# A two-block transformer kernel on one core: no masked quarter in the window attention, projections placed inside other waits, and 24 instead of 20 up projections ahead of the one-hot rounds

## The chip, the cores and the metric

One core of a Trainium2 chip runs the whole program in one launch. The metric is the time of the device from start to end of that launch, in microseconds (us), as the median of several runs. The engines are TensorE (PE, with its weight loads as PEld), VectorE (DVE), ScalarE (ACT), GpSimd (POOL) and SyncE (SP), which here only issues transfers.

## The reference, cut to what matters

All tensors are float32, 256 tokens, width 1024. Two blocks follow each other.

```
first block:  h = x + gmlp(rms_norm(x))                 # u, v, g: 3 x 2048 columns; v mixed over time; 2048 -> 1024
              k, v = split(rms_norm(h) @ w_kv + b_kv)    # 2 key/value heads of 64, k with rotary
              q, g = split(rms_norm(h) @ w_in)           # 16 query heads of 64
              scores: 128-token chunks, keys of the own and the previous chunk,
                      key valid if 0 <= q - k < 128;  m = max(scores, sink)
              p = exp(s - m) / (sum + exp(sink - m));  h += (p @ v * silu(g)) @ w_out
              h = rms_norm(h, final)
second block: h1 = rmsnorm(h) * (1 + sc1) + sh1          # sc, sh, g from silu(c) @ ada_w + ada_b
              q, k, v = h1 @ w_in; 16 heads of window and dilated attention with a bias table
              h += g1 * (rmsnorm(o) @ w_out)
              peer(h2): q = h2 @ wq, two 128-key scores per head, top 16 x 16 -> top 16 of 8 heads
                        a = h2 . u[id],  w = gate * gelu(a),  y = sum of w * v[id] over 16384 experts
              out = rmsnorm(h + g2 * y)
```

## The kernel before, in words

Activations are kept with features on the partitions and the 256 tokens in the free dimension. All weights come in one stream of 128 x 1024 float32 chunks (512 KB), through a ring of four slots `raw`, `WH`, `WL`. SP loads a chunk; `hi` on ACT (L397) copies it, rounded, to WH; `lo` on DVE (L799; `pool_low` on POOL, L1539, for some) writes the rest, raw - WH, to WL. Slot c is written again once chunk c - 4 is finished. Each product is three products of halves, hi x hi, hi x lo, lo x hi. `feature_tile` (L1567) does one chunk: 8 k-slices x 3 matmuls = 24 matmuls of 256 tokens, with the weight as the stationary side. `token_tiles` (L1567 too) has the activations as the stationary side and gives tokens on the partitions. Each engine's order is written out by hand; waits are counts on semaphores (`up(c, g, per)` is such a count in a loop).

The stages in order, with their names in the code:

- `ug_step`, `aout_step`: the first mixer. `aout_step` ends with the residual x and, for each k-slice, the gained inputs X1 (for keys and values) and X2 (for queries).
- Keys and values: chunk C_KV by `feature_tile` into keys, the sum of squares by `spread` (a plain float32 product with ones), chunk C_KV + 1 by `token_tiles`, `rms` on DVE, `rope_in`/`rope_out`, `vB`.
- `swa_step(m)`, m = 0..10, one pair of heads each, skewed: PE makes the query tile (bank m % 2), `scores` of pair m - 1 (L1694), `values` of pair m - 2 (L1716), the gate tile, `rope_turn`, `turn_probs` of pair m - 1 (L1706) and `turn_out` of pair m - 2. DVE has `soft_in`: scale and mask (L995), the maximum (L1000), three operations on 4 columns (L1004, L1006, L1009). ACT has `exps` (L511) and `pt_out` (L521). Scores are 128 x 256 for each head and each half of the queries; queries of the first half have no key in the second.
- `out_steps`: w_out, 8 chunks (C_BOUT). Then `spread` of two sums of squares (POOL adds the squares, L1514), the norm on DVE, `modulated`: F = x * gain * R and X1H/X1L.
- `v2_step`: the values of the second block, 8 chunks (C_V2), as token tiles into vC. `mix_step(m)`: as `swa_step`, with keys of their own and a bias table, then C_COUT, C_WQ with the key scores and DVE's `top16`.
- `early_up` (PE), `early_step` (ACT, hi and Gelu): the first TOP = 20 up projections of the 128 columns of experts. DVE in this time makes the lists of chosen experts; ACT has one Exp for their gates (L691). `lists_ready` lets PE turn the lists (L1920).
- 32 rounds: 8 one-hot products (L1934) and one up projection each. Then EARLY = TOP + 32 down projections (`down`, L1953), then LATE = 128 - EARLY columns, each an up (L1967, L1969) and a down projection.

## Time and profile before

| what | value |
|---|---|
| median of 3 runs | 1405.53 us (1404.94 to 1407.23) |
| profiled execution, its own time | 1403.09 us |
| its span | 1401.3 us |
| PE, DVE, ACT, POOL busy | 94%, 71%, 54%, 27% |
| mean granted clock of TensorE | 0.969 of full speed |
| transfers | 249.21 MB, 177 GB/s read over the span |

Busy is the share of the span in which an engine had an instruction of the program under way. Matmuls overlap, so a mean time of one is longer than the distance from one to the next. The granted clock is 1 where TensorE ran at 2.4 GHz, 0.5 where at 1.2 GHz.

### The profile page before, as it was taken

Reading aid. Unit: us, or ns where it says so; the run is one execution under the profiler, and the core shown is the slowest. Engines: PE = TensorE matmul, PEld = TensorE weight load, DVE = VectorE, ACT = ScalarE, POOL = GpSimd, SP = SyncE. Lnnn points to the kernel's source line nnn. Section 1 sums busy time; section 2 is a strip of 40 time slices with the busy share of each in tenths; the row PEclk is TensorE's granted clock in tenths of the full one; section 3 lists DMA queues with packets and bytes.
Section 4 is the critical chain, followed back from the end, with each engine's and each line's share of the span. In section 5 each row is a group of like instructions: output and inputs, shape, how many; then the busy total and the mean of one; then the engine's idle time right before and its main releaser. Section 6 shows DMA issues by size and latency. Waiting matters only on the chain.

```text
span 1401.3 us, 26798 instructions
## 1 busy us (share of the span) xinstructions
PE 1314.0 (94%) x8582; PEld 1184.8 (85%) x8582; DVE 997.7 (71%) x1847; ACT 760.5 (54%) x1260; POOL 372.7 (27%) x252
## 2 busy tenths in 40 slices
PE   6999998997789888998999999999999999999996
PEld 6999998887689788998999967777888888888885
DVE  6799988884567686797788845555666666666666
ACT  6344453554445545545988844444555555555553
POOL 1089812112231024786777700000000000000000
PEclk9999999998899889998999999999999999999998
DMA  9877784442365533453333345555756556565561
GB/s 337 316 247 263 242 271 164 141 151 79 130 196 186 175 106 136 160 178 127 110 118 111 116 151 180 180 180 180 240 184 192 191 181 189 188 192 181 192 188 67
DMA packets 68024, 249.21 MB, mean 178 GB/s; under 512 B 7808, under 2 KB 8192, under 8 KB 67200
## 3 DMA queue, kind: packets, MB, share of 16 engines
q1 hardware_dynamic: 58896, 214.80, 46.5%
q10 hardware_dynamic: 9072, 33.69, 7.1%
q8 instruction: 33, 0.54, 0.2%
q14 instruction: 23, 0.19, 0.1%
HBM read 245.83 MB, written 2.62 MB: 177 GB/s over the span
## 4 chain that ended last, share of the span: by engine, by line
PE 81%; DVE 9%; ACT 4%; issue 3%; DMA 2%; POOL 1%; ACTq 0%; DVEq 0%; SPq 0%; POOLq 0%
PE ps L1567 30%; PE ps L1953 26%; PE ps L1967 10%; PE ps L1969 5%; PE ps L1934 4%; ACT pr L511 2%; PE ps L1706 1%; DVE small L1000 1%; DVE s L995 1%; PE ps L1842 1%; DMA ada<-adaT 1%; DVE WL L799 1%; PE ps L1716 1%; DMA raw<-stream 1%; PE ps L1694 1%
## 5 line engine op out<-in xcount | busy, mean ns | idle before, releaser
L799 DVE TENSOR_TENSOR WL<-raw,WH 128x1024 fp32r<-128x1024 f32 x326 | 412.3, 1268 | 174.7 <-ACT WH L397 171.6
L397 ACT ACTIVATE WH<-raw 128x1024 fp32r<-128x1024 f32 x394 | 414.4, 1055 | 178.1 <-PE ps L1953 85.3
L1567 PE MATMUL ps<-X,WH 128*128 128x256 f32 x1840 | 347.3, 290 | 6.1 <-DVE X2L L919 4.1
L1567 PEld LDWEIGHTS ps<-X,WH 128*128 128x128 f32 x1840 | 292.1, 196 | 7.3 <-DVE X2L L919 4.3
L1567 PE MATMUL ps<-X,WL 128*128 128x256 f32 x920 | 263.5, 286 | 0.0
L1967 PE MATMUL ps<-X,WH 128*128 128x512 f32 x608 | 216.9, 397 | 0.0
L1953 PE MATMUL ps<-WH,wvH 128*128 128x512 f32 x512 | 207.5, 405 | 2.6 <-DVE wvL L1337 2.4
L1953 PE MATMUL ps<-WH,wvL 128*128 128x512 f32 x512 | 202.5, 396 | 0.0
L1953 PE MATMUL ps<-WL,wvH 128*128 128x512 f32 x512 | 202.0, 395 | 0.0
L1539 POOL TENSOR_TENSOR WL<-raw,WH 128x1024 fp32r<-128x1024 f32 x68 | 164.0, 2413 | 82.5 <-ACT WH L397 82.5
L1567 PEld LDWEIGHTS ps<-X,WL 128*128 128x128 f32 x920 | 179.1, 195 | 0.0
L1969 PE MATMUL ps<-X,WL 128*128 128x256 f32 x608 | 170.5, 280 | 0.0
L1967 PEld LDWEIGHTS ps<-X,WH 128*128 128x128 f32 x608 | 114.2, 188 | 27.6
L1953 PEld LDWEIGHTS ps<-WH,wvH 128*128 128x128 f32 x512 | 96.9, 189 | 39.7 <-DVE wvL L1337 15.6
L1969 PEld LDWEIGHTS ps<-X,WL 128*128 128x128 f32 x608 | 114.7, 189 | 2.9
L1953 PEld LDWEIGHTS ps<-WH,wvL 128*128 128x128 f32 x512 | 96.5, 188 | 22.4
L1953 PEld LDWEIGHTS ps<-WL,wvH 128*128 128x128 f32 x512 | 96.8, 189 | 17.4
L747 ACT ACTIVATE tmp<-tmp 128x256 f32<-128x256 f32 x76 | 31.7, 418 | 107.2 <-DVE tmp L1346 107.2
L1354 DVE TENSOR_TENSOR tmp<-tmp,A 128x256 f32<-128x256 f32 x76 | 32.3, 425 | 51.9 <-ACT tmp L747 51.9
L1567 PE MATMUL ps<-WH,X 128*128 128x256 f32 (+1 forms) x352 | 64.4, 284 | 3.6 <-DVE WL L799 3.6
L1567 PE MATMUL ps<-YH,WH 128*128 128x256 f32 x224 | 64.1, 286 | 3.0 <-DVE YL L882 3.0
L807 DVE CUSTOM_DVE_ANT_0 ada<-ada,cb 128x1024 f32<-128x1024 f32 x48 | 60.7, 1265 | 6.7 <-DMA ada<-adaT 3.5
(262 smaller groups left out, 2185.6 us busy)
## 6 DMA issues: line engine op xcount, KB each, us to landing
raw<-stream SPq DMA_DIRECT2D x394, 512.0 KB, 3.4
ada<-adaT ACTq DMA_DIRECT2D x48, 512.0 KB, 4.2
bias<-att_bias ACTq DMA_DIRECT2D x9, 512.0 KB, 4.5
x<-xT SPq DMA_DIRECT2D x2, 512.0 KB, 6.7
ws<-wsT SPq DMA_DIRECT2D x1, 1024.0 KB, 11.6
lng<-rows SPq DMA_DIRECT2D x1, 1024.0 KB, 8.1
lnb<-rows SPq DMA_DIRECT2D x1, 1024.0 KB, 7.1
bsb<-rows SPq DMA_DIRECT2D x1, 1024.0 KB, 8.1
```

The costliest lines, as they stand in the source:

```text
L397: act.activation(WH[:, slot, :], raw[:, slot, :], ACT.Copy).then_inc(h_done, 1)
L511: act.activation(pr[:, k, :], s[:, k, :], ACT.Exp, bias=negm[:, k:k + 1], accum_out=small_den[:, par, k:k + 1]).then_inc(p_ready, 1)
L747: act.activation(tmp[i % 2][:, :], tmp[i % 2][:, :], ACT.Gelu).then_inc(gelu_ready, 1)
L799: dve.tensor_tensor(WL[:, slot, :], raw[:, slot, :], WH[:, slot, :].bitcast(F32), ALU.subtract).then_inc(l_done, 1)
L807: dve.tensor_tensor_reduce(ada[:, n % 2, :], ada[:, n % 2, :], cb[:, :], 1.0, 0.0, ALU.mult, ALU.add, st2).then_inc(ada_sum, 1)
L1354: dve.tensor_tensor(tmp[2 + i % 2][:, :].unsqueeze(1), tmp[i % 2][:, :].unsqueeze(1), tiles(A, EARLY + i, g, 2), ALU.mult).then_inc(w_read ...
L1539: pool.tensor_tensor(WL[:, slot, :], raw[:, slot, :], WH[:, slot, :].bitcast(F32), ALU.subtract).then_inc(l_done, 1)
L1567: mm = pe.matmul(out_ap, a(kc), b(kc), start=(first and kc == 0 and i == 0), stop=(last and kc == KC - 1 and i == 2))
L1934: mm = pe.matmul(ps[:, gate_bank(e) + half, k * P:(k + 1) * P], O1[:, n, :], (O2a, O2b[:, e % 2])[half][:, k, :], start=True, stop=True)
L1953: mm = pe.matmul(ps[:, 4 + 2 * t + h, :], a[:, j % 2, ts_], b[:, slot, hs], start=(first and i == 0), stop=(last and i == 2), skip_group_c ...
L1967: pe.matmul(ps[:, i % 2, :].rearrange("p (x t) -> p x t", x=2), wh(kc), X1[:, :, kc, :], start=(kc == 0), stop=False, skip_group_check=True)
L1969: mm = pe.matmul(ps[:, i % 2, 0:T], wl(kc), X1H[:, kc, :], start=False, stop=(kc == KC - 1), skip_group_check=True)
```

## The change

It has six parts.

1. `TOP` is 24. The last of the 24 up projections stands behind the turning of the lists; ACT's Exp stands after the 16th Gelu instead of after the last.
2. The window attention of the first block leaves out the keys of the second half for the queries of the first: `scores`, mask, exp, `turn_probs` (6 blocks of 128 instead of 8) and `values` (6 products instead of 8). In both attentions the sign of the scores is turned in the scaling (minimum instead of maximum, Exp with scale -1), which leaves out one operation on 4 columns. The bias of the next query stands between scaling and minimum.
3. The key tile starts k-slice by k-slice. The value tile of the first block is a feature tile in `swa_step(1)`, turned by two transposes.
4. w_out of the first block is cut in parts (`out_part`), which stand between the last steps of the attention.
5. The values of the second block are projected from the input before its norm is known (XGH/XGL, 258 columns: 256 tokens and the shift twice), as feature tiles into vF, turned by 16 transposes, scaled by the norm's factor on ACT (`v_token`); the shift's product is added to the attention's output. The norm is worked out beside. The transposes of tiles 4 to 6 stand in `mix_step(0)`, the eighth value tile in `mix_step(1)`, its transposes in `mix_step(2)`.
6. The order of the chunks in the stream follows (`place`), and the loops of these parts are written out.

```diff
-TOP = 20
+TOP = 24
@@ PE, keys of the first block @@
-            feature_tile(C_KV, None, 6, X1H, X1L)
-            spread(1, sacc_done, KC, tmp[5][:, :])
-            token_tiles(C_KV + 1, None, 5, X1H, X1L, 1)
+            for kc in range(KC):
+                pe.wait_ge(xl_ready, KC + 2 * kc + 1)
+                for i, (a, b) in enumerate(((wh, X1H), (wh, X1L), (wl, X1H))):
+                    mm = pe.matmul(ps[:, 6, 0:T], a(kc), b[:, kc, :], start=(kc == 0 and i == 0), stop=(kc == KC - 1 and i == 2))
+            spread(1, sacc_done, KC, tmp[5][:, :])
 ...
+            def out_part(n, k0, k1):
+                if k0 == 0:
+                    pe.wait_ge(l_done, C_BOUT + n + 1)
+                for kc in range(k0, k1):
+                    pe.wait_ge(yl_ready, AG + kc + 1)
+                    for i, (a, b) in enumerate(((wh, YH), (wh, YL), (wl, YH))):
+                        mm = pe.matmul(ps[:, bout_bank(n), 0:T], a(kc), b[:, 1 + kc, :],
+                                       start=(kc == 0 and i == 0), stop=(kc == KC - 1 and i == 2))
+            def turn_v():
+                pe.wait_ge(vt_ready, 1)
+                for t in range(NT):
+                    mm = pe.transpose(ps[:, 2, T + t * P:T + (t + 1) * P], tmp[1][:, t * P:(t + 1) * P], ident)
@@ PE, swa_step(m) @@
+                if m == 8:
+                    pe.wait_ge(rope_s, 8)
+                    out_part(0, 0, 4)
                 if 1 <= m <= 8:
                     ...
-                    scores(m - 1, g, 0)
+                    scores(m - 1, g, 0, True)
                 ...
-                    feature_tile(C_QG + 2 * m + 1, g, 2 + m % 2, X2H, X2L)
+                    feature_tile(qg_chunk(m) + 1, g, 2 + m % 2, X2H, X2L)
+                    if m == 0:
+                        rope_turn(0, 6)
                     rope_turn(m + 1, m % 2, g)
+                if m == 1:
+                    pe.wait_ge(gr_ready, AG + 1)
+                    feature_tile(VB_CHUNK, None, 2, X1H, X1L)
+                if m == 8:
+                    pe.wait_ge(rope_s, 9)
+                    out_part(1, 0, 4)
+                    pe.wait_ge(s_ready, 8)
+                    out_part(2, 0, 4)
+                    for n in range(3):
+                        out_part(n, 4, 5)
                 if 1 <= m <= 8:
-                    turn_probs(m - 1, g)
+                    turn_probs(m - 1, g, 3)
+                if m == 1:
+                    turn_v()
+                if m == 9:
+                    for n in range(3):
+                        out_part(n, 6, 7)
                 if m >= 2:
                     turn_out(m - 2, g)
+                if m == 8:
+                    for n in range(3):
+                        out_part(n, 5, 6)
 ...
+            out_part(3, 0, 5)
+            for n in range(3):
+                out_part(n, 7, 8)
+            out_part(3, 5, 8)
+            for n in range(4, 8):
+                out_part(n, 0, KC)
@@ DVE, swa_step and soft_in @@
+                if m == 1:
+                    dve.wait_ge(chunk_done, VB_CHUNK + 1)
+                    link(dve.tensor_tensor(tmp[1][:, :], ps[:, 2, 0:T], R[:, 1, :], ALU.mult))
+                    dve.tensor_scalar(tmp[1][:, :], tmp[1][:, :], vec[:, V_BV:V_BV + 1], None, ALU.add)
+                dve.scalar_tensor_tensor(out=s_h[:, :, 0:n], in0=ps[:, 4:6, 0:n], scalar=-HD ** -0.5, in1=b,
+                                         op0=ALU.mult, op1=ALU.subtract).then_inc(s_ready, 1)
+                if between is not None:
+                    between()
 ...
+                dve.tensor_reduce(negm_h[:, :, 1], s_h[:, :, P:3 * P], AX_X, ALU.min).then_inc(mx_ready, 1)
+                dve.tensor_reduce(negm_h[:, :, 0], s_h[:, :, 0:P], AX_X, ALU.min).then_inc(near_ready, 1)
@@ ACT, swa_step @@
-                    hi(C_QG + 4 + 2 * m, g)
+                    if m != 1:
+                        hi(C_QG + 4 + 2 * m, g)
 ...
+                if m == 1:
+                    hi(C_QG + 6)
@@ DVE and ACT, each chunk n of w_out @@
+                dve.tensor_tensor(x[:, n, :], x[:, n, :], ps[:, bout_bank(n), 0:T], ALU.add)
+                dve.tensor_scalar(tmp[n % 2][:, :], x[:, n, :], s1[:, n:n + 1], None, ALU.mult)
+                act.activation(XGH[:, n, 0:T], tmp[n % 2][:, :], ACT.Copy)
...
+                dve.tensor_tensor(XGL[:, n, 0:T], tmp[n % 2][:, :], XGH[:, n, 0:T].bitcast(F32), ALU.subtract)
@@ PE, values of the second block @@
+            def v2_tile(n, bank):
...
+                        mm = pe.matmul(ps[:, bank, 0:T + 2], a(kc), b[:, kc, :], start=(kc == 0 and i == 0),
+                                       stop=(kc == KC - 1 and i == 2))
...
+            for n in range(7):
...
+                v2_tile(n, 1 + n % 3)
+                if n == 1:
+                    spread(2, sacc_done, 24, tmp[5][:, :])
+                    spread(3, sacc_done, 24, tmp[2][:, :], at0=T)
+                if n == 4:
+                    pe.wait_ge(r_ready, 3)
+                    turn_row(R[:, 0, :])
+                if n == 5:
+                    v2_turn(0, 4)
+                    v2_turn(1, 5)
+                if n == 6:
+                    pe.wait_ge(v_out, 20)
+                    v2_turn(2, 4)
+                    v2_turn(3, 5)
@@ PE and ACT, up projections ahead of the rounds @@
-            fours(pe, TOP, early_up)
+            fours(pe, TOP - 4, early_up)
+            for j in range(TOP - 4, TOP - 1):
+                early_up(j)
             pe.wait_ge(lists_ready, 1)
...
+            early_up(TOP - 1)
-            fours(act, TOP, early_step)
+            fours(act, TOP - 8, early_step)
             act.wait_ge(exp_in, 1)
             act.activation(best[:, :, :], best[:, :, :], ACT.Exp).then_inc(exp_ready, 1)
+            for j in range(TOP - 8, TOP - 1):
+                early_step(j)
```

## Rows read from the trace of the kernel before

**Rows 1.** The page: busy time by engine; the chain that ended last, by engine.

```profile
PE 1314.0 (94%) x8582; PEld 1184.8 (85%) x8582; DVE 997.7 (71%) x1847; ACT 760.5 (54%) x1260; POOL 372.7 (27%) x252
...
PE 81%; DVE 9%; ACT 4%; issue 3%; DMA 2%; POOL 1%; ACTq 0%; DVEq 0%; SPq 0%; POOLq 0%
```

**Rows 2.** The waits of PE: who for whom: us in total, times, longest us.

```profile
PE ps L1706 <- ACT pr L511: 17.4, 12, 4.8
...
PE ps L1789 <- DVE X L1107: 6.6, 1, 6.6
```

**Rows 3.** Windows: stretch, us, busy us of each engine, granted clock, DMA share, GB/s.

```profile
215.70:249.10 33.40, 26.19 (x197) 24.69 (x197) 26.63 (x52) 12.93 (x23) 7.75 (x8) 0.95 0.45 144
258.30:313.30 55.00, 52.48 (x421) 48.00 (x421) 48.44 (x101) 29.98 (x76) 10.57 (x10) 1.00 0.43 143
314.40:357.00 42.60, 34.67 (x246) 32.83 (x244) 20.66 (x34) 18.78 (x38) 16.32 (x16) 0.84 0.30 99
357.00:394.90 37.90, 27.78 (x196) 26.51 (x196) 19.50 (x31) 16.27 (x29) 2.60 (x5) 0.82 0.40 132
394.90:413.70 18.80, 14.71 (x113) 14.01 (x113) 15.47 (x22) 8.96 (x16) 7.15 (x7) 0.93 0.60 197
647.40:662.40 15.00, 8.94 (x49) 8.58 (x50) 7.92 (x14) 9.04 (x12) 6.40 (x5) 0.66 0.27 94
809.20:963.90 154.70, 154.68 (x625) 114.87 (x626) 80.80 (x103) 69.58 (x102) 0.00 (x0) 0.99 0.51 173
```

**Rows 4.** The chain by time, the last step of that attention.

```profile
325.72 3.66 PE ps L1716 x16
```

**Rows 5.** The chain by time, the lists and the first rounds.

```profile
647.87 1.28 ACT L691
...
649.16 0.42 ACT best L691
...
662.34 1.78 PE ps L1934 x16
664.12 2.88 PE ps L1567 x24
```

**Rows 6.** Groups by shape, the value tile of the first block (224.6 to 230.2): busy, mean ns.

```profile
L1567 PE MATMUL ps<-WH,X 128*128 128x128 f32 x32 | 5.7, 279 | 0.0
```

**Rows 7.** The chain by time, one step of the window attention.

```profile
280.14 1.10 PE ps L1706 x8
...
285.75 1.23 DVE s L995
```

**Rows 8.** The chain by time, at the keys: start us, us, what.

```profile
219.84 4.63 PE ps L1567 x24
224.47 0.45 PE ps L1602 x2
...
232.39 5.99 PE ps L1567 x48
```

**Rows 9.** Groups by shape, five such steps (258.3 to 313.3): busy, mean ns, idle before.

```profile
L799 DVE TENSOR_TENSOR WL<-raw,WH 128x1024 fp32r<-128x1024 f32 x10 | 12.2, 1220 | 3.5 <-ACT WH L397 3.5
...
L511 ACT ACTIVATE pr<-s,small 128x256 f32<-128x256 f32 x20 | 9.9, 497 | 16.5 <-DVE small L1009 16.5
...
L1000 DVE TENSOR_REDUCE small<-s 128x4 f32<-128x1024 f32 x5 | 6.1, 1220 | 0.2
...
L962 DVE TENSOR_SCALAR qb<-tmp,vec 128x256 f32<-128x256 f32 x5 | 1.8, 353 | 1.1 <-DVE tmp L958 1.1
```

**Rows 10.** The chain by time, the first step of the second attention.

```profile
402.74 1.67 DVE R L1172
```

**Rows 11.** Timeline of DVE, the end of the lists: start us, us, line, operation.

```profile
646.04 0.41 DVE L1276 CAST i<-ps 128x256 f32<-128x256 uint32 x1
```

**Rows 12.** The chain by time, two of the late columns (over 70 such distances).

```profile
975.40 2.77 PE ps L1953 x12
980.98 2.78 PE ps L1953 x12
```

More of the change, by code:

```diff
@@ L63, with qg_chunk, qk_chunk, v2_chunk @@
 NCAND = sum(ROWS)
+def qg_chunk(m):
+    return C_QG + 2 * m - (m < 2)
+def qk_chunk(m):
+    return C_QK + 2 * m - (m < 2)
+def v2_chunk(n):
+    return C_V2 + n if n < 7 else C_QK + 3
+VB_CHUNK = C_QG + 3
 class Chain:
@@ L301, in load, with place @@
                 if g is None:
-                    sp.dma_start(raw[:, slot, :], stream[c]).then_inc(raw_in[slot], 16)
+                    sp.dma_start(raw[:, slot, :], stream[place(c)]).then_inc(raw_in[slot], 16)
                 else:
                     sp.dma_start(raw[:, slot:slot + 1, :], group[j][:, bass.ds(g, 1), :]).then_inc(raw_in[slot], 16)
+            def place(c):
+                for first, last in ((C_KV + 1, VB_CHUNK), (C_QK - 1, C_QK + 3)):
+                    if first <= c <= last:
+                        return first if c == last else c + 1
+                return c
             def groups(c, n):
@@ L336, in _, with load_groups, load_moved @@
             rounds = NCHUNK // RING
-            cs = groups(RING * first, rounds - first)
-            with sp.Fori(0, rounds - first) as g:
-                for j in range(RING):
-                    load(RING * first + j, g, cs, j)
+            def load_groups(k0, k1):
+                cs = groups(RING * k0, k1 - k0)
+                with sp.Fori(0, k1 - k0) as g:
+                    for j in range(RING):
+                        load(RING * k0 + j, g, cs, j)
+            def load_moved(k0, k1):
+                for c in range(RING * k0, RING * k1):
+                    load(c)
+            load_groups(first, C_KV // RING)
+            load_moved(C_KV // RING, C_KV // RING + 2)
+            load_groups(C_KV // RING + 2, C_QK // RING)
+            load_moved(C_QK // RING, C_QK // RING + 2)
+            load_groups(C_QK // RING + 2, rounds)
             for c in range(RING * rounds, NCHUNK):
@@ L509, in exps, with pt_out @@
                     act.wait_ge(rc_ready, up(p - 1, g, 2))
-                for k in range(4):
-                    act.activation(pr[:, k, :], s[:, k, :], ACT.Exp, bias=negm[:, k:k + 1],
-                                   accum_out=small_den[:, par, k:k + 1]).then_inc(p_ready, 1)
+                for h in range(2):
+                    for t in range(NT):
+                        k = 2 * h + t
+                        keys = (slice(0, P), slice(P, 3 * P))[t] if sinks else slice(t * T, (t + 1) * T)
+                        act.activation(pr_h[:, h, keys], s_h[:, h, keys], ACT.Exp, bias=negm[:, k:k + 1], scale=-1.0,
+                                       accum_out=small_den[:, par, k:k + 1]).then_inc(p_ready, 1)
                 if sinks:
                     act.activation(small_es[:, par, :], dsk, ACT.Exp).then_inc(es_ready, 1)
-            def pt_out(p, g):
+            def pt_out(p, g, blocks):
                 act.wait_ge(pt_mm, up(p + 1, g, 2))
@@ L1115, in modulated, with between_tiles @@
                         low(kc - 1)
+                    after(kc)
                 low(KC - 1)
-            modulated(0, s1, mod[:, 0:8], R[:, 0, :])
-            def v2_step(q, g):
-                lo(C_V2 + 2 * q + 3, g)
-                lo(C_V2 + 2 * q + 4, g)
-            with dve.Fori(0, 2) as g:
-                for q in range(2):
-                    v2_step(q, g)
+            def between_tiles(kc):
+                if kc == 2:
+                    lo(C_V2 + 6)
+                if kc == 4:
+                    rms_tokens(1)
+                if kc == 5:
+                    lo(C_V2 + 7)
+            modulated(0, s1, mod[:, 0:8], R[:, 0, :], between_tiles)
+            for n in range(8, 11):
+                lo(C_V2 + n)
             def normed(n):
@@ L1688, in rope_turn, with scores @@
                 pe.matmul(ps[:, bank, T:2 * T], perm, qb[:, i % 2, :], start=True, stop=True).then_inc(rope_mm, 1)
-            def scores(p, g, kslot):
+            def scores(p, g, kslot, near=False):
                 for h in range(2):
@@ L1767, in _ @@
             steps(pe, swa_step)
-            def out_steps(c, count, x0):
-                pe.wait_ge(yl_ready, count)
-                with pe.Fori(0, 2) as g:
-                    for n in range(4):
-                        pe.wait_ge(x_ready, up(x0 + n - 1, g, 4))
-                        feature_tile(c + n, g, n % 2, YH, YL)
-            out_steps(C_BOUT, AG + 8, 8)
-            spread(2, sacc_done, 24, tmp[5][:, :])
-            spread(3, sacc_done, 24, tmp[2][:, :], at0=T)
-            pe.wait_ge(l_done, C_V2 + 2)
@@ L1782, in _ @@
-            wh, wl = weight(WH, C_V2 % RING, 2), weight(WL, C_V2 % RING, 2)
-            for kc in range(KC):
-                pe.wait_ge(xl_ready, 3 * KC + kc + 1)
-                for t in range(NT):
-                    o = ps[:, t, 0:2 * P].rearrange("p (a n) -> p a n", a=2)
-                    xh, xl = X1H[:, kc, t * P:(t + 1) * P], X1L[:, kc, t * P:(t + 1) * P]
-                    for i, (a, b) in enumerate(((xh, wh), (xh, wl), (xl, wh))):
-                        mm = pe.matmul(o, a, b(kc), start=(kc == 0 and i == 0), stop=(kc == KC - 1 and i == 2))
```

358 lines of the change are left out of this document (237 added, 121 removed).

## The prediction, before the change was run

> **What bounds the kernel now.** I read the page first. PE is busy 94% of the span and holds 81% of the chain that ended last; DVE follows with 9% [rows 1]. So time comes back where PE has less to do, where it waits, or where it runs at the lower clock after waiting. The waits of PE come next: the largest is for the exponentials, 17.4 us in 12 waits; one for the norm between the blocks has 6.6 [rows 2]. The windows show where they lie. Width less busy time is PE's idle time: 7.2 us at the keys and the first pair, 2.5 in five steady steps of the window attention, 7.9 from its last step to the end of w_out, 10.1 at the norm and the value projections, 4.1 at the first step of the second attention, 6.1 at the lists. The clock there is 0.95, 1.00, 0.84, 0.82, 0.93 and 0.66 [rows 3]: waits were followed by work at 1.2 GHz. So the work behind a wait is dear as well: the values of the last pair took 3.66 us for 16 matmuls [rows 4], 0.23 each.
>
> **Prices of PE.** Nothing is stalled in a tile of 24 matmuls of 256 columns: 2.88 us, 0.12 each [rows 5]. The token tile of the first block has 48 matmuls of 128 columns in the 5.7 us between 224.6 and 230.2 (these are 32 of them) [rows 6], 0.12 each too: fewer columns are no cheaper here. A turning matmul of 128 columns costs 1.10/8 = 0.137 [rows 7]. A values matmul of 64 columns I take at 0.12, as the others; a scores matmul of 128 columns likewise saves nothing.
>
> **Keys, value tile, first pair.** The key tile started at 219.84 and took 4.63, partly at the low clock; the query tiles came at 232.39 [rows 8]. Now six slices run from 215.8, the last two as their inputs come, to 219.9; the spread ends near 221. DVE still does one `lo` first, so its norm begins near 222.1 instead of 224.9 (2.8 earlier). Meanwhile PE has two tiles. Then a new wait: `rope_turn(1)` stands for the query's rotation behind `rope_turn(0)`, and DVE has two `lo` (1.22 each, [rows 9]) before it. I get 230.6, 3 us idle, and the second pair's query tile at 231 instead of 238.4. The value tile fills the wait for the first exponentials (2.88 against 1.8), but `turn_v` brings another: DVE reaches it only behind the `lo` of chunk C_QG + 6, whose `hi` now stands behind the exponentials on ACT. ACT 2.0 of exps, 1.06, DVE 1.22, three operations of 0.42 and two more: 2.5 us idle. What is left at the second pair's turning is 4.1 us. Ends: 1.5 (the clock falls in both new waits, and POOL's rotation is late) to 6.5 (`turn_v` finds its input).
>
> **Steady steps.** The step from 280.14 is not bound by PE. Its chain goes from the turning over the copy to pT, `hi`, `lo` (1.22), the gate product, the scale, query bias, mask (from 285.75), maximum (1.22), three small operations and four exps back to the turning, 11.0 us later [rows 7, 9]. PE's own work in it is 10.5: 52.48 in 5 steps [rows 3]. The change takes 2 turning matmuls (0.27) and 4 values matmuls (a float32 product is 2 instructions: 0.48) from PE: 9.8. From the chain it takes 0.27 of turning, 0.2 of copy, about 0.3 each of mask and maximum (768 for 1024 elements; the maximum in two pieces, so 0.25), one small operation (0.2), 0.2 of exps, and the 0.26 that the query bias waited before the mask (1.1 in five steps less the plain distance): 1.7, so 9.3. PE takes over as the bound at 9.8, with DVE at some 9.3 of work behind it. I take 9.9: 5 x (11.0 - 9.9) = 5.5 us. Ends: 2 (DVE's load decides, 10.6) and 7 (scores against 128 keys are cheaper too, which the token tile speaks against).
>
> **Last pair and w_out.** From the end of the last steady turning (314.4) to the end of w_out (357.0) are 42.6 us [rows 3]. The new order on PE: scores 1.07, values 1.45, turning 0.82, values 1.45, two `turn_out` 0.54, w_out 8 x 2.88 = 23.0; 28.4. Of the waits I keep 0.7 at the fifth chunk: its slot comes free only when the first chunk ends, then `hi` 1.06 and `lo` 1.22, against 1.8 us of tail pieces; and 0.3 at the last slice of y. In between the pieces cover: 5.4 us of work against a softmax of about 5, 1.35 against the copy to pT. Sum 29.4; gain 13.2, of which I take 12.5 for slips. Ends: 8 (the ring waits repeat at each of four chunks: ACT has `hi`, a rounded copy and two squares, 2.3 us of 2.88) and 13.5.
>
> By the Trainium skill (TensorE: Matmul & The Clock Gate, Terms) the penalty is the throttled time times the share of the clock taken away. Clock 0.84 over 42.6 us would be 13.6 us at half and 6.8 us of penalty; width less idle less work at full clock (30.0 of 34.7 busy, with the masked quarter) gives 4.7. The rows decide, since part of the throttled time is idle; by the rule the gain would be 2 us larger.
>
> **Norm and second values.** From 357.0 to the end of the first turning of the second attention (413.7, in which the 0.93 window lies) are 56.7 us [rows 3]. New: 7 value tiles, 20.2; two spreads 0.45, one turned row 0.27, 8 transposes 1.1. Beside it DVE: spreads end at 6.3 after w_out, two sums, a `lo`, square root (with its table 1.28, [rows 5]), reciprocal 1.67 [rows 10] and Newton to 12.6, `modulated` with two `lo` to 22.3. The last wait is ACT's: it has F's copies, `hi` and square root before `v_token`, so the second pair of transposes waits 1.6 us at 21.6. The key/query tile starts at 23.8 instead of 37.9. In the next steps the DVE row is longer than before: the norm of the first block (3.4 us, from the reciprocal at 402.74, [rows 10]) still stands before the first mask, and `ks` is 2.5 us later, since `lo` of the chunk waits for the tile before. So the turning comes 19.9 us after the tile (before 17.1), with the eighth tile (2.9) and three pairs of transposes inside: 43.7, with the turning at the low clock 45.7. Gain 11.0, less 0.6 for a wait on vF and a pair of transposes in the following step: 10.4. Ends: 5 (each `hi` on ACT late by 0.7) and 13. The 258-column matmul has no row before; the distance of 256 columns is 0.12, that of 512 in the down projections 154.7/624 = 0.25 [rows 3]. I take the nearer end, 0.121, so 0.2 us in all; the other end is 0.13 x 192 = 25 us dearer, and alone would end at 1389.
>
> **Later steps of the second attention.** One small operation less in each softmax: PE's waits there, 1.0 in four steps and the last, shrink by 0.9 (0 to 1.2).
>
> **24 up projections.** Before, the 20 tiles end at 647.4; ACT loads a table (1.28), the exponential and the lists follow, and round 1 starts at 662.34, 15 us later with one round done [rows 5, 3]. Now Exp is done before DVE's lists are (646.4, [rows 11]), the lists are ready at 647.6, PE turns them behind the 23rd tile (656.0, 0.8), the 24th tile covers the way over ACT, POOL and DVE: round 0 at 659.7, round 1 at 664.9 with 0.5 of wait: 2.6 us later with four tiles more. These four cost 2.98 each in the down projections (154.7/52, [rows 3]), 11.9, and save four late columns of 5.58 [rows 12], 22.3. DVE's product over 32 more elements lies in rounds of 4.66 that PE bounds [rows 5]. Net 22.3 - 11.9 - 2.6 = 7.8; ends 5 (round 0 waits as long as before) and 8.5.
>
> By the Trainium skill (ScalarE: Activation LUTs, What ACT_TABLE_LOAD costs) a switch is 1.28 us of load and 1.38 of drain. Exp between two Gelus needs two switches: by the row 2 x 1.28 + 0.42 lies in ACT's slack of two tiles and costs nothing; by the page 5.7 us, and the 19th tile would start some 1.8 us late. The rows have the load from 647.87 and Exp at 649.16, right behind it [rows 5], so I count nothing.
>
> **The sum.** 4.1 + 5.5 + 12.5 + 10.4 + 0.9 + 7.8 = 41.2. The profiled execution's own time is 1403.1 (span 1401.3 and 1.8 around it); less 41.2 is 1361.9. The median of the runs lies 2.4 above that execution, so against it the same sum gives 1364.3. I say 1364.
>
> **Rivals.**
> (A) The engines beside PE take over. In four of the covers ACT or DVE has 80% or more of a tile's time. Then each part gives its lower end: 1.5 + 2 + 8 + 5 + 0 + 5 = 21.5, so 1384. For it: DVE is already 88% busy in the steady steps (48.44 of 55 us) [rows 3]. Against it: ACT is at 30 of 55 there.
> (B) All covers hold and the clock never falls: upper ends, 6.5 + 7 + 13.5 + 13 + 1.2 + 8.5 = 49.7, so 1356.
> (C) Slower. The 258-column products leave the fast form and run like the plain float32 product of the spread, 0.45 for 256 columns [rows 8], instead of 0.12: 192 x 0.33 = 63 us more, 1427. It decides from 0.21 us more on each. For it: no other product has such a row length. Against: both halves are of the same rounded type.
> (D) The change does not do what it says: the moved stretches wait for the same `lo` as before, and only the removed matmuls (8 x 0.75 and 2.9 of the value tile) and the up projections (7.8) count: 1389.
>
> **How the numbers follow.** Forecast 0.60, its own range 1358 to 1375; A 0.22; B 0.09; C 0.04; D 0.05. Below 1355 lies the part of B with more luck than I can name, above 1387 C and D. Range 1355 to 1387. A measurement of this kernel tells 0.2% (3 us) from no change. Faster is all but C and a rest of D: 0.94; same 0.01; slower 0.05.
>
> **What would show it.** Steady steps at 9.9 us with almost no wait for the exps; under 9.7 or over 10.5 my bound is wrong. No low clock between the last turning and the eighth value tile; w_out ending 29 to 31 us after that turning. A wait of 2 to 3 us at `turn_v` and of 3 at `rope_turn(1)`. A wait of 3 to 4 us for the first exps of the second attention. Matmuls of 258 columns 0.12 apart. Round 1 some 17.5 us after the 20th tile, with four tiles more. The prediction is wrong if the stretch from 357 to 413.7 doesn't shrink by 8 us or more, or if the parts shrink and the end does not follow.

## The result, and the profile after

| what | before | after |
|---|---|---|
| median of the runs | 1405.82 us (1404.94 to 1407.23, 4 runs) | 1369.06 us (1365.56 to 1373.99, 4 runs) |
| ratio | | 0.974, 95% interval 0.970 to 0.978 |
| profiled execution, its span | 1401.3 us | 1363.8 us |

The change made the kernel 2.6% faster. The forecast was 1364, with a range of 1355 to 1387. The sum of its parts was 41.2 us; between the two profiled spans lie 37.5 (the profiled execution of the kernel after was the shortest of its four), between the medians 36.8.

First the page of the kernel after: busy time by engine, then the chain that ended last, by engine.

```profile
PE 1296.6 (95%) x8560; PEld 1170.5 (86%) x8560; DVE 992.1 (73%) x1846; ACT 759.0 (56%) x1281; POOL 386.1 (28%) x256
...
PE 63%; POOL 6%; issue 4%; DVE 3%; ACT 2%; ACTq 0%; POOLq 0%; DVEq 0%
```

PE's busy time fell by 17.4 us against [rows 1], less than half of the 37.5. Work at 1.2 GHz counts as busy, so it lies within the 17.4; the other 20.1 are waits that went. The shares of the chain add up to 78% only: the profile follows it back to 304 us and shows no piece of it before, so its 63% is not to be set against the 81% of [rows 1].

Next the windows of these stages (columns as in [rows 3]; pairs are counted from 0). Their edges are landmarks of PE's order: the keys' last slices to the turning of pair 1, five steady steps, turning of the last pair (7) to w_out's end, from there to the key/query tile, from there to the first turned probabilities of the second attention, turning of the lists to round 1, the 56 early down projections. The first, third and sixth have other edges than those of [rows 3].

```profile
219.20:256.40 37.20, 30.30 (x220) 27.59 (x221) 30.31 (x61) 17.00 (x35) 8.84 (x8) 0.95 0.42 143
256.40:305.10 48.70, 47.91 (x391) 43.81 (x390) 44.57 (x100) 27.61 (x76) 10.63 (x10) 1.00 0.49 162
314.40:335.20 20.80, 20.11 (x171) 19.90 (x170) 15.55 (x27) 13.47 (x26) 11.99 (x11) 1.00 0.31 102
335.20:365.10 29.90, 24.48 (x185) 23.54 (x183) 24.80 (x42) 20.67 (x40) 8.16 (x9) 0.94 0.54 181
365.10:385.70 20.60, 17.57 (x144) 16.64 (x142) 13.04 (x17) 11.52 (x27) 6.34 (x7) 1.00 0.64 205
626.80:637.20 10.40, 8.67 (x72) 8.31 (x71) 6.41 (x10) 6.80 (x10) 8.14 (x6) 1.00 0.41 141
783.90:948.60 164.70, 164.51 (x672) 122.31 (x673) 87.03 (x111) 75.40 (x111) 0.00 (x0) 1.00 0.52 175
```

The two stretches that the table below needs besides are, first in the kernel before, from the start of the key tile to the turning of pair 1, then in the kernel after, from the end of the last steady turning (pair 6) to w_out's end:

```profile
219.80:258.30 38.50, 35.32 (x268) 32.97 (x268) 31.19 (x56) 16.54 (x33) 7.55 (x8) 0.96 0.41 131
305.70:335.20 29.50, 28.32 (x239) 27.59 (x238) 22.55 (x45) 17.98 (x40) 13.80 (x12) 1.00 0.33 112
```

The steady steps and the stretch to w_out's end are nearly full and at full clock. Most idle time is left in three windows: 6.9, 5.4 and 3.0 us; ahead of round 1 there are 1.7. The waits of PE in these (215 to 400, columns as in [rows 2]) name who is late:

```profile
PE ps L1963 <- DVE XGL L1204: 3.8, 3, 2.1
PE ps L1844 <- ACT pr L564: 3.6, 3, 3.0
PE ps L1827 <- DVE qb L1060: 3.3, 2, 2.9
PE ps L1882 <- DVE tmp L1177: 3.0, 1, 3.0
PE ps L1970 <- ACT vC L645: 1.6, 1, 1.6
```

L1844 is `turn_probs`, L1827 `rope_turn`, L1882 `turn_v`, L1970 `v2_turn`: these four were forecast, nearly to the number. L1963, `v2_tile` waiting for the lower half of its input, was not. It waits three times inside the first value tile (PE's timeline, then DVE's last XGL):

```profile
338.64 0.38 PE L1963 MATMUL ps<-XGH,WH 128*128 128x258 f32 x1 [1.45 <-DVE XGL L1204]
...
341.38 0.39 PE L1963 MATMUL ps<-XGH,WH 128*128 128x258 f32 x1 [2.12 <-DVE XGL L1204]
...
342.25 0.58 PE L1963 MATMUL ps<-XGH,WH 128*128 128x258 f32 x1 [0.24 <-DVE XGL L1204]
...
341.47 0.72 DVE L1204 TENSOR_TENSOR XGL<-tmp,XGH 128x256 fp32r<-128x256 f32 x1 [0.15 <-ACT XGH L618]
```

Part by part, from the same landmarks in both traces:

| part | forecast | measured | |
|---|---|---|---|
| keys, value tile, first pair | 4.1 | 1.9 | turning of pair 1 at 258.32, now 256.43 (the mixer before it ended 0.4 later, so 2.3 from its end) |
| five steady steps | 5.5 | 6.3 | 55.0, now 48.7 |
| last pair and w_out | 12.5 | 13.1 | 42.6, now 29.5 from the end of the turning |
| norm and second values | 10.4 | 6.4 | 56.7, now 50.3 (to 385.5, where the turning has its last matmul under way; the window above ends 0.2 later) |
| later steps | 0.9 | 1.1 | |
| 24 up projections | 7.8 | 8.5 | first round 3.9 later, rounds 0.2 shorter, downs 10.2 longer, late columns 22.4 shorter; of the downs 1.5 are the clock of the kernel before, see below |
| sum | 41.2 | 37.3 | |

### The profile page after: what moved, and what is told of

Read it like the earlier page. It is cut to its first block, busy times and chain, and to the rows that moved or that the text cites. A ratio compares the mean times of both kernels' runs of the same rounds, so it can differ in the third digit from the quotient of the medians.

```text
span 1363.8 us, 26648 instructions
## 1 busy us (share of the span) xinstructions
PE 1296.6 (95%) x8560; PEld 1170.5 (86%) x8560; DVE 992.1 (73%) x1846; ACT 759.0 (56%) x1281; POOL 386.1 (28%) x256
## 4 chain that ended last, share of the span: by engine, by line
PE 63%; POOL 6%; issue 4%; DVE 3%; ACT 2%; ACTq 0%; POOLq 0%; DVEq 0%
PE ps L2183 27%; PE ps L1701 10%; PE ps L2197 10%; POOL WL L1673 5%; PE ps L2199 5%; PE ps L2164 4%; PE ps L1874 1%; PE ps L1963 1%; PE ps L1855 1%; PE ps L2070 1%; PE ps L1844 1%; ACT pr L564 1%; PE ps L1834 1%; DVE WL L893 0%; DVE small L1096 0%
## 5 line engine op out<-in xcount | busy, mean ns | idle before, releaser
L447 ACT ACTIVATE WH<-raw 128x1024 fp32r<-128x1024 f32 x394 | 413.7, 1055 | 160.0 <-PE ps L2183 89.6
L1701 PE MATMUL ps<-X,WH 128*128 128x256 f32 x1888 | 354.0, 289 | 2.7 <-DVE WL L893 1.9
L2197 PE MATMUL ps<-X,WH 128*128 128x512 f32 x576 | 205.5, 397 | 0.0
L1673 POOL TENSOR_TENSOR WL<-raw,WH 128x1024 fp32r<-128x1024 f32 x72 | 173.6, 2415 | 81.5 <-ACT WH L447 81.4
L2183 PEld LDWEIGHTS ps<-WH,wvL 128*128 128x128 f32 x512 | 96.2, 188 | 22.3
L1439 DVE TENSOR_TENSOR O<-idio,ps 128x512 f32<-128x512 f32 x64 | 43.8, 684 | 25.6 <-PE ps L2164 17.0
L1494 DVE TENSOR_TENSOR wvL<-tmp,wvH 128x256 fp32r<-128x256 f32 x72 | 30.6, 425 | 40.9 <-ACT wvH L846 40.9
## 6 DMA issues: line engine op xcount, KB each, us to landing
ws<-wsT SPq DMA_DIRECT2D x1, 1024.0 KB, 11.5
```

Source lines behind the costliest of these rows:

```text
L447: act.activation(WH[:, slot, :], raw[:, slot, :], ACT.Copy).then_inc(h_done, 1)
L1439: dve.tensor_tensor(O1[:, 4 * half:4 * half + 4, :], iota4, of_four(i1_l, e, half), ALU.is_equal).then_inc(eq_ready, 1)
L1494: dve.tensor_tensor(wvL[:, i % 2, :], tmp[2 + i % 2][:, :], wvH[:, i % 2, :].bitcast(F32), ALU.subtract).then_inc(wl_ready, 1)
L1673: pool.tensor_tensor(WL[:, slot, :], raw[:, slot, :], WH[:, slot, :].bitcast(F32), ALU.subtract).then_inc(l_done, 1)
L1701: mm = pe.matmul(out_ap, a(kc), b(kc), start=(first and kc == 0 and i == 0), stop=(last and kc == KC - 1 and i == 2))
L2183: mm = pe.matmul(ps[:, 4 + 2 * t + h, :], a[:, j % 2, ts_], b[:, slot, hs], start=(first and i == 0), stop=(last and i == 2), skip_group_c ...
```

## The experiments

Eight kernels, each run five times beside the kernel before, in two series that have their own runs of the kernel before. The kernel after was not run in them. By its own ratio of 0.974 it would be at 1367.6 in the first series (numbers 1, 2, 4, 6) and 1368.1 in the second; that is the value to compare with. The interval of its ratio, 0.970 to 0.978, makes that some 1363 to 1373, and of the eight medians only those of numbers 6 and 8 lie outside. So for most of them the total tells little, and the argument rests on the stretches in the traces. Even these begin at different times: in the eight traces of the family whose code is the same up to there (all but number 6) the key tile starts at 215.7 to 218.4 us.

**1. No sum of squares on POOL (e1_no_sum).** In w_out's loop on POOL:

```
-  pool.tensor_tensor(acc[:, :], acc[:, :], square[:, :], ALU.add)
+  pool.tensor_tensor(acc[:, 0:1], acc[:, 0:1], square[:, 0:1], ALU.add)
```

> Leaves out the summing of w_out's squares on POOL: the 16 additions between w_out's chunks take one column of 256, so the statistics of the norm are wrong; all waits and all other work stay. Theory 1 (POOL slows DVE): in the changed kernel lo took 1.76 us beside these additions and 1.22 elsewhere, and DVE, a serial loop of 2.77 us per chunk, finished the eighth chunk 4.8 us after PE. With the additions gone lo is back at 1.22, the loop at 2.2 us, XGL of the last chunk comes near 338.3 instead of 341.5, the first value tile waits 0.5 us or less instead of 3.8, the lower clock behind the wait (1.4 us lost) goes, and the whole is 3.5 to 5 us below the changed kernel: near 1364. Rival 1 (the loop is bound by ACT's hi, rounded copy and two squares, 2.4 us a chunk, or by the ring): lo returns to 1.22 but XGL stays behind ACT, the wait stays over 2.5 us and the whole within 1.5 us of the changed kernel. Rival 2 (lo is slow for another reason, ACT's writes or the DMA): lo stays at 1.7 and nothing changes.

Measured: 1362.91 us (1360.84 to 1365.72), ratio 0.970 (0.968 to 0.971). DVE's timeline, first in the kernel after, one chunk of w_out (start us, us, line, operation):

```profile
324.36 0.41 DVE L1204 TENSOR_TENSOR XGL<-tmp,XGH 128x256 fp32r<-128x256 f32 x1
324.69 1.76 DVE L893 TENSOR_TENSOR WL<-raw,WH 128x1024 fp32r<-128x1024 f32 x1
326.37 0.41 DVE L1211 TENSOR_TENSOR x<-x,ps 128x256 f32<-128x256 f32 x1
326.82 0.38 DVE L1213 TENSOR_SCALAR tmp<-x,small 128x256 f32<-128x256 f32 x1
```

and in the kernel without these additions, the same four:

```profile
327.68 0.42 DVE L1204 TENSOR_TENSOR XGL<-tmp,XGH 128x256 fp32r<-128x256 f32 x1
328.02 1.22 DVE L893 TENSOR_TENSOR WL<-raw,WH 128x1024 fp32r<-128x1024 f32 x1
329.15 0.41 DVE L1211 TENSOR_TENSOR x<-x,ps 128x256 f32<-128x256 f32 x1
329.61 0.35 DVE L1213 TENSOR_SCALAR tmp<-x,small 128x256 f32<-128x256 f32 x1
```

There is no idle time between these rows: DVE is a serial loop, 2.77 us a chunk with POOL beside it, 2.19 without. `lo` carries 0.54 of the 0.58. ACT doesn't hold the loop: in the kernel after, ACT itself is idle for 0.38 us a chunk ahead of XGH, until DVE's product is there. The window from w_out's end to the key/query tile, in this kernel:

```profile
338.60:363.30 24.70, 22.72 (x183) 22.05 (x182) 20.96 (x38) 18.21 (x37) 1.48 (x5) 1.00 0.58 198
```

24.7 instead of 29.9 us, the clock back at 1.00, and of the wait for XGL 0.37 us is left. The forecast had 23.8 for it. Theory 1 holds in mechanism and, by the trace, in size; both rivals fall.

**2. The gain in ACT's rounded copy (e4_gain_in_copy).**

```
-  dve.tensor_scalar(tmp[n % 2][:, :], x[:, n, :], s1[:, n:n + 1], None, ALU.mult)
-  act.activation(XGH[:, n, 0:T], tmp[n % 2][:, :], ACT.Copy)
-  dve.tensor_tensor(XGL[:, n, 0:T], tmp[n % 2][:, :], XGH[:, n, 0:T].bitcast(F32), ALU.subtract)
+  act.activation(XGH[:, n, 0:T], x[:, n, :], ACT.Copy, scale=s1[:, n:n + 1])
+  dve.scalar_tensor_tensor(out=XGL[:, n, 0:T], in0=x[:, n, :], scalar=s1[:, n:n + 1],
+                           in1=XGH[:, n, 0:T].bitcast(F32), op0=ALU.mult, op1=ALU.subtract)
```

> The whole computation, another form of one step: ACT makes the rounded part as copy of x times the gain, and DVE the rest as x times gain less the rounded part, so the product on DVE (0.38 us a chunk) and one hop go. Theory 1 (DVE's loop decides): the loop is 2.77 - 0.31 = 2.46 us a chunk, XGL of the last chunk comes 2.5 us earlier, the wait of 3.8 us falls to 1.5 or less and the low clock behind it mostly goes: 2.5 to 4 us below the changed kernel. Rival (ACT decides: its hi, copy, two squares and the wait for POOL's slot are 2.7 us a chunk): the loop stays at 2.7 us, the wait over 3 us, and the whole within 1 us.

Measured: 1367.81 us (1365.31 to 1370.75), ratio 0.973 (0.972 to 0.975): the total tells nothing. In the trace the wait for XGL is 2.1 instead of 3.8 us and the window from w_out's end to the key/query tile 28.0 instead of 29.9. DVE's timeline there:

```profile
329.07 0.42 DVE L1212 TENSOR_TENSOR x<-x,ps 128x256 f32<-128x256 f32 x1
...
331.63 0.41 DVE L1212 TENSOR_TENSOR x<-x,ps 128x256 f32<-128x256 f32 x1
331.96 0.63 DVE L1204 SCALAR_TENSOR_TENSOR XGL<-x,small,XGH 128x256 fp32r<-128x256 f32 x1
332.51 1.76 DVE L893 TENSOR_TENSOR WL<-raw,WH 128x1024 fp32r<-128x1024 f32 x1
```

The loop is 2.56 us (329.07 to 331.63), not 2.46: the fused operation takes 0.63 where the subtraction took 0.41. Its form explains 0.07 of that (the same form takes 0.48 in `modulated`, where POOL is idle), POOL beside it the rest. The low clock still comes (0.94). The stretch is 1.9 shorter, where 2.5 to 4 were expected of the whole: in the direction of the theory, less in size; ACT isn't the bound.

**3. The late lo (e6_lo_late).** `lo(C_V2 + 2)` moved behind the last XGL.

> The whole computation; only the lo of chunk C_V2 + 2 is moved on DVE, from ahead of w_out's eighth chunk to behind the last XGL. It is 1.76 us in a loop that ends 4.8 us after PE. Theory (DVE's serial loop decides when the last slices come): the eighth addition, gain and XGL come 1.7 us earlier, of 3.8 us of wait 1.9 to 2.3 stay, and the stretch from w_out's end to the key/query tile is 1.7 to 3 us shorter (more if the low clock does not come). Rival (ACT's hi and copies hold the last XGL): 0.5 us or less. In the total this is hard to tell from nothing; the stretch in the trace decides.

Measured: 1366.75 us (1364.11 to 1368.99), ratio 0.973 (0.971 to 0.974). The waits for XGL are 1.45, 0.45 and 0.26, 2.2 us in all, and the window is 27.6 us at clock 1.00, 2.3 shorter. The theory's stretch came; the total can't show it.

**4. 20 up projections in the new order (e2_top20).** `TOP = 20`, all else as after.

> The changed kernel with 20 instead of 24 up projections ahead of the one-hot rounds, its order otherwise kept. The prediction had 7.8 us for this part (22.3 for four late columns, less 11.9 for their down projections, less 2.6 for a later start). The two traces give 22.35 - 10.2 (56 downs against 52) - 3.9 + 0.2 = 8.4. If that is right, this kernel is 7.5 to 8.5 us above the changed one (near 1377). Rival: Exp's new place between the Gelus, not the four tiles, carries part of it; then the stretch from the 20th tile to round 1, 15 us before, is already shorter here (12.5 us) and the difference is 5 to 6 us.

Measured: 1371.05 us (1369.25 to 1371.61), ratio 0.975 (0.974 to 0.977): 3.4 us above the kernel after, not 8 (its own interval reaches up to 5 above that point, so the total alone does not show the 3.4). This expectation, and with it the forecast's account of the part, was wrong. From the last key scores to round 1 the kernel before has 70.3 us, this one 67.5, the kernel after 74.2 with four tiles of 2.9 more. So Exp's place between the Gelus and the 20th tile behind the turning, which no run tells apart, bring 2.8 with no further tile. The window from the 19th tile's end to round 1, here:

```profile
617.60:632.70 15.10, 10.98 (x72) 10.97 (x72) 10.43 (x19) 7.29 (x10) 8.41 (x6) 0.77 0.28 93
```

PE still waits 4.1 us for the lists and then works at the lower clock. Four tiles more are 11.6 us of work for 6.7 of time: they cover 4.9. Their own worth is 22.35 - 11.73 - 6.70 = 3.9 in the traces, and 3.4 in the medians. The four downs are priced here between two traces with no low clock in the down stretch: 11.73, as forecast (11.9). The 10.2 of the table is less because the kernel before had 3.4 us at the lower clock at its first downs, which cost 1.5, and the kernel after had none. The rival was right that the order carries a part, and too high in its 5 to 6.

**5. 28 up projections (e7_top28).** `TOP = 28`.

> The changed kernel with 28 up projections ahead of the one-hot rounds. From 20 to 24 the two traces gave 22.36 us for four late columns, less 11.74 for four more in the down stretch, less 6.7 for a later first round (four tiles of 2.9 covered 4.8 us of wait and low clock): 3.9. From 24 on nothing before the turning of the lists is left to cover, so four more cost all of 11.6: 22.4 - 11.7 - 11.6, that is 0.9 us above the changed kernel, within its noise. Rival: the number of tiles itself pays (a late column costs more than an early up projection and a down together), and the gain goes on with 3 us or more.

Measured: 1369.05 us (1368.76 to 1371.12), ratio 0.975 (0.974 to 0.977). The turning of the lists waited for nothing in the kernel after, and four tiles more cost their 11.5 us in full; the down stretch is 11.8 longer (against number 6's, whose first downs ran at the lower clock as these did; against that of the kernel after, which had none, 13.4), the late columns 22.3 shorter: 1.0 slower by the traces, 0.9 by the medians. The count pays only as far as it covers a wait.

**6. The masked quarter again (e3_full_mask).** Four turned blocks, 256 keys, one minimum over 1024 elements, values over both halves:

```
-  turn_probs(m - 1, g, 3)
+  turn_probs(m - 1, g, 4)
-  scores(m - 1, g, 0, True)
+  scores(m - 1, g, 0)
```

> The changed kernel with the masked quarter computed again (two turning matmuls, four values matmuls, scores over 256 keys, mask and exps over 1024 elements, one minimum of 1.22 us instead of 0.68 and 0.41). Prediction: the steady step is PE's, so the quarter costs PE's 0.27 + 0.48 and the steps are at 10.6 to 10.7 us, 5 us more over eight pairs. Theory now: scores against 128 keys were cheaper too (0.86 against 1.07), so 0.96 more a step, steps at 10.7, and with first and last pair 6 to 7.5 us above the changed kernel. Rival: the chain over DVE decides as it did before the change, the step goes back to 11.0 with a wait of 0.3 us or more for the exps, and the whole is 9 to 11 us above.

Measured: 1377.58 us (1374.36 to 1380.54), ratio 0.981 (0.979 to 0.983). The five steady steps:

```profile
257.90:311.60 53.70, 52.42 (x421) 47.98 (x420) 47.14 (x96) 29.88 (x76) 10.64 (x10) 1.00 0.44 146
```

10.74 a step against 9.74 after and 11.0 before; PE is busy 52.4 of 53.7. What is left is the wait for the exponentials (257.9 to 311.7, with the wait ahead of the sixth turning; columns as in [rows 2]):

```profile
PE ps L1842 <- ACT pr L564: 1.3, 4, 0.5
```

In the stretch that answers to it that wait is 0.6 in the kernel after and 2.4 in the kernel before. So of the 1.26 that a step gained, 1.0 is the quarter's (0.9 of it PE's work, 0.1 wait) and 0.26 the shorter chain's. From the keys' last slices to the first turning of the second attention the trace is 8.6 us longer (173.9 for 165.3), of which up to 1.1 is more time at the lower clock in the first pair: the rest is the theory's upper end. The medians say 10. So the rival's size is about met, and its cause in a small part only: with the quarter, the chain over DVE and ACT holds PE for 0.26 us a step on the mean, under the rival's 0.3, and PE's work is the rest. The last 2 us between trace and medians stay open; they are less than the interval of the kernel after.

**7. DVE's order at the first pair (e5_first_pair).** At step 0 the query's scale and bias stand ahead of three `lo`, its sine and the gate product ahead of two of them, at step 1 the value tile's operations ahead of one (shortened; the lines are sketched):

```
 if m == 0:
+    rope_scale(1, 0); rope_bias(1, ...); rope_out(0, 6)
+    lo(C_KV + 4)
+    gr2 product; rope_out(1, 0)
+    lo(C_QG + 3); lo(C_QG + 4)
 if m == 1:
     gr2 product; rope_out(2, 1); value tile's product and bias
+    lo(C_QG + 6)
```

> The whole computation; DVE's order at the first pair alone is other: the query's scale, bias and sine of pair 0 and the gate product stand ahead of three lo instead of behind them, and at step 1 the gate product, the sine and the two operations of the value tile stand ahead of the lo of chunk C_QG + 6. Theory: the waits of 2.9 us at rope_turn(1) and 3.0 at turn_v are these lo and nothing else; both fall below 0.7 us, a wait of 1 us or so for POOL's rotation takes the place of the first, and the low clock behind them (4.7 us for a tile of 3.1) goes. The turning of pair 1 comes 5 to 7 us earlier after the first key slice. The same code gave that turning at 256.4, 258.6, 259.9 and 262.0 in four profiles, with one to four stretches at the low clock, so the spread between executions should shrink too: 1362 to 1364, with 3 us or less between the lowest and highest. Rival: these waits only stand for the next ones (scores wait for POOL's rotation, the turning for the exponentials, all in one chain), the turning comes 2 us earlier or less, and the whole within 2 us of the changed kernel (near 1367.5).

Measured: 1364.14 us (1361.72 to 1365.37), ratio 0.971 (0.970 to 0.972). PE's timeline in the kernel after, the two waits (idle before and its releaser in brackets):

```profile
231.38 0.70 PE L1827 MATMUL ps<-qb,cBt 128*128 128x256 f32 x2 [2.90 <-DVE qb L1060]
...
247.62 0.44 PE L1882 MATMUL ps<-idio,tmp 128*128 128x128 f32 x2 [3.03 <-DVE tmp L1177]
```

and in this kernel, all waits of PE in the stretch from `rope_turn(1)` on:

```profile
230.36 0.70 PE L1838 MATMUL ps<-qb,cBt 128*128 128x256 f32 x2 [0.26 <-DVE qb L1060]
234.79 0.93 PE L1845 MATMUL ps<-ks,qs 64*128 64x128 f32 x8 [0.85 <-POOL qs L1639]
239.81 0.70 PE L1838 MATMUL ps<-qb,cBt 128*128 128x256 f32 x2 [1.06 <-DVE qb L1060]
244.29 0.44 PE L1893 MATMUL ps<-idio,tmp 128*128 128x128 f32 x2 [0.25 <-DVE tmp L1187]
```

5.9 us of wait became 2.4, and the window that answers to 219.20:256.40 is

```profile
220.90:253.30 32.40, 29.07 (x221) 26.07 (x221) 29.84 (x60) 16.79 (x35) 7.87 (x8) 1.00 0.50 163
```

32.4 us at full clock. With the order of the kernel after, six profiles (the kernel after and numbers 1 to 5) have 37.2 to 41.0 us for the same stretch: 3.4 us at the lower clock in two of them, 6.8 in three, and twice 6.8 in the one of 41.0. Here, and in number 8, none came. The theory holds in its waits and its clock; the turning comes 4.8 us earlier than in the trace of the kernel after, just under the 5 to 7 expected, and 4.8 to 8.6 earlier than in the six. That the runs spread less is not shown: 3.7 us here and 8.4 in the kernel after, but 2.4 in numbers 4 and 5, whose first pair is the old one.

**8. All orders together (e8_all).** Numbers 2, 3 and 7, and two more:

```
 # DVE: reciprocal and Newton of the first block's root
-  at the end of mix_step(0)
+  in mix_step(1), behind soft_in(8, g, False)
 # POOL
+  distance(0); distance(1)
   the last pool_low ahead of the rounds
-  distance(0); distance(1)
```

> The whole computation with all the orders together: the first pair's order on DVE; w_out's gain in ACT's rounded copy and the late lo of C_V2 + 2; the reciprocal and Newton of the first block's root behind the first mask and minimum of the second attention; both distances on POOL ahead of the last pool_low. Theory by stretches, against the changed kernel: first pair 5 to 7; norm 3.5 to 5 (waits of 3.8 to under 0.7 and no low clock); the first exponentials of the second attention come 3.0 us earlier (wait of 3.03 to under 0.5) and the low clock behind them goes, 3 to 4.5; round 0 loses its wait of 1.47: 1.2 to 1.5. Sum 13 to 18, so 1350 to 1356. Rival: DVE and ACT have no room there, each wait comes back one step later (ks, the exponentials of the second pair, XR on POOL), and the sum is under 8: 1360 or more.

Measured: 1353.36 us (1351.96 to 1356.01), ratio 0.963 (0.962 to 0.965), the fastest of all; near 15 below the kernel after, and clear of its interval. Its windows answer to the first, third, fourth, fifth and sixth of the kernel after:

```profile
219.40:251.80 32.40, 29.07 (x221) 26.05 (x221) 29.85 (x60) 16.80 (x35) 7.87 (x8) 1.00 0.49 158
309.80:330.60 20.80, 20.10 (x171) 19.90 (x170) 15.42 (x23) 14.45 (x28) 11.76 (x12) 1.00 0.33 104
330.60:358.30 27.70, 24.56 (x184) 23.62 (x183) 23.98 (x38) 19.98 (x38) 6.78 (x8) 0.94 0.57 194
358.30:374.80 16.50, 16.50 (x138) 15.84 (x136) 11.90 (x14) 10.47 (x26) 0.00 (x0) 1.00 0.70 224
616.50:625.50 9.00, 8.56 (x72) 8.22 (x70) 6.86 (x11) 7.01 (x10) 8.24 (x6) 1.00 0.47 160
```

First pair 4.8 us; norm 2.2, where 3.5 to 5 were expected (`lo` still takes 1.75 beside POOL, 1.5 us of wait remain and the clock still falls once); the first turning of the second attention 3.05 earlier with no wait left, the tile behind it at full clock (3.10 instead of 4.61); round 0 1.3. The parts add up to 12.9. They are as expected but for the norm and, by 0.2, the first pair. The two profiled spans differ by 9.5 only; there the kernel after caught a good execution (3.5 under its median), this one its worst.

## Why the prediction was right, and where it was off

**The bound.** Right: PE's work, waits and clock gave the whole gain, and the two full stretches, the steady steps and the last pair with w_out, came within 0.8 us of their terms.

**Its own signs.** Most stood: 9.74 us a step, w_out's end 29.5 after the turning, waits of 3.0 at `turn_v`, 2.9 at `rope_turn(1)` and 3.0 for the first exponentials, 258 columns 0.12 apart. Three did not. The clock fell between the last turning and the eighth value tile (at 341.9). Round 1 came 19.1 us after the 20th tile, not 17.5. And the stretch from 357 to 413.7 shrank by 6.4 us, where the prediction had called itself wrong under 8. So the total came out, and the account of that stretch failed by the prediction's own test.

**Luck in the sum.** The measured parts miss theirs by 2.2 and 4.0 on one side and by 0.8, 0.6, 0.2 and 0.7 on the other, which is partly cancellation. The last of these is chance: 1.5 us of that part come from the clock at the first downs, which was low in the profile of the kernel before and not in that of the kernel after.

**Steady steps.** 9.74 for 9.9. The step taken wrong was "a scores matmul of 128 columns likewise saves nothing": the four scores products, two of them now over 128 keys, took 0.86 instead of 1.07, so each of the two saved 0.11. The row that spoke against it, the token tile, was of rounded halves over 128 rows; the scores are plain float32 over 64. Which of the two makes the difference no run tells. Experiment 6 shows the rest as argued: nine tenths of the quarter are PE's work, and with it back the chain holds PE for only 0.26 us a step.

**Last pair and w_out.** 29.5 for 29.4, with the ring's wait at the fifth chunk at 0.69 for 0.7. The 0.3 at the last slice of y did not come; in its place PE stood 0.48 ahead of the last scores for POOL's rotation, which the sum didn't have, and the scores were 0.2 cheaper. The allowance of 0.7 for slips wasn't needed.

**Norm and second values: the mis-sized term, 6.4 for 10.4.** The mechanism was right (24 matmuls of 258 columns take 2.9, the `v_token` wait 1.61 for 1.6, the wait ahead of the first turning 3.03, between the 3 and 4 named). The step that failed is "7 value tiles, 20.2", which let the first of them run through from w_out's end. I had asked of ACT whether it keeps up with w_out (2.3 of 2.88 us), not of DVE. Four chunks end nearly together, DVE has only then begun, and at 2.77 us a chunk it gains 0.1 on PE's 2.88: its eighth XGL began 6.2 us after w_out's end (341.47). That costs 3.8 of wait and about 1.4 at the lower clock (27 matmuls in 4.84 us). Experiment 1 takes out 5.1 and lands 0.9 from the forecast of 23.8. The key/query tile came 6.1 us late by this, the part only 4.0: the turning started 0.4 earlier after that tile than forecast and took 1.1 less, at full clock (the low clock came behind it, where the tile took 4.61), and the 0.6 for a wait in the following step did not come. Rival A had this mechanism. It struck here (6.4 between its 5 and the forecast's 10.4) and, as `lo` ahead of PE's inputs, in the first pair (1.9, near its 1.5).

**First pair, 1.9 for 4.1.** Both waits stood as forecast, 2.9 for 3 and 3.03 for 2.5. Not counted was their clock: the q tile behind the first took 4.71 us. The prediction put that in the lower end (1.5), though it had itself read that waits are followed by work at 1.2 GHz [rows 3]. In experiment 7 the waits go and no low clock comes.

**24 up projections, 8.5 for 7.8.** Right in sum only. "2.6 us later" was 3.9: round 0 waited 1.47 us for ACT's half of the one-hots, since POOL's `distance` stood behind a `pool_low` of 2.4; experiment 8 takes it out. Against it, the down projections seem 1.7 cheaper than priced, but 1.5 of that is the clock in the profile of the kernel before; without it the part is 7.0. And "four tiles" were not all that paid: 3.9 us are theirs, 2.8 the order's (experiments 4 and 5).

**A table switch.** Two loads of 1.28 us stand around Exp, at 607.38 and 610.06, with Exp at 608.68 and the next Gelu at 611.35, each right behind its load, and PE has no wait there. By the Trainium skill (ScalarE: Activation LUTs, What ACT_TABLE_LOAD costs) each has a drain of 1.38 besides; this trace shows none.

**Rivals.** (A) held in the two parts named. (B) fell by waits, (C) by 0.12 us between 258-column matmuls, (D) by full covers.

**Not settled.** Why the clock falls in one execution and not in another, with the same waits. In six of the nine profiles of this family 3.4 us at the lower clock lay at the first down projections and cost 1.6 us; the kernel after had none in its profile, the kernel before had it.

## What to carry to other kernels

When PE's work is packed tighter, add up for every helper engine, and not only the busiest, the serial time of one chunk with the durations it has beside its neighbours, and start it where its first input comes: an engine at 96% of PE's time per chunk made up 0.1 us a chunk of its late start. Ahead of an operation for which PE stands, no bulk operation that could be a few places later: such moves gave here near 15 us of 1368. Tiles put ahead of a wait pay only up to its length; find that length from a version with fewer.

## What the runs showed of the hardware

**DVE and POOL block each other.** `lo`, with both inputs in SBUF, took 1.76 us beside POOL's additions and 1.22 without; the fused operation 0.63, and 0.48 where POOL was idle. The residual addition, with one input in PSUM, stayed at 0.41 and the one with a single tensor input at 0.38 for 0.35. It goes both ways. Of POOL's additions those started while `lo` ran took 1.60 us, those started together with XGL's subtraction 1.00, and the last, with DVE idle until its last 0.16 us, 0.73. One that began at 324.36 ended at 325.37, `lo` from 324.69 ended 0.54 late, and the next addition, from 325.45, ended at 327.05, near 0.9 late. XGL's subtraction has two SBUF inputs as well and yet stayed at 0.41 (seven of eight): each time it began less than 0.01 us before an addition, and the addition paid. The eighth, started while an addition ran, took 0.72. By the Trainium skill (SBUF — State Buffer, Who interferes with whom) a DVE operation with two SBUF inputs contends with a GpSimd operation that reads SBUF, and the order of issue decides who blocks; these rows agree, both in which operations suffer and in who pays.

**A wait can cost more than its length.** Behind the wait of 2.9 us at `rope_turn(1)` a tile took 4.71 instead of 3.10, behind that of 3.03 in the second attention 4.61. It doesn't come every time: behind the same wait of 2.9 at `rope_turn(1)` the tile took 3.20 in number 4, and after the 3.0 at `turn_v` the tile took 3.09 in the kernel after and 5.47 in that of number 2, with the same code.
